# Layer norm output in four steps, and stage-end norms in row halves on two engines

## What is computed

```python
# first block (one layer)
h = h + y @ w_out[l]                       # y: two self attentions of rmsnorm(h), each normed
h = h + memory_cross_attention(rmsnorm(h, g_cross[l]), rmsnorm(mem, g_mem[l]), ...)
h = h + conv_ffn(rmsnorm(h, g_ffn[l]), ...)
# second block, per layer and stream
def conformer_conv(a, conv_w, conv_b, norm_g, norm_b, w_o):
    gl = a[..., :CONV_WIDTH_2] * jax.nn.sigmoid(a[..., CONV_WIDTH_2:])
    y = lax.conv_general_dilated(gl, ...) + conv_b
    y = jax.nn.silu(layer_norm(y, norm_g, norm_b))
    return y @ w_o
...
x = x + g1 * rms_norm(y, mix_post_g[l])    # y: the three branches merged, @ w_out
h2 = modulate(rms_norm(x, ffn_pre_g[l]), sh2, sc2)
x = x + g2 * rms_norm(sq_relu_mlp(h2, w_ff1[l], w_ff2[l]), ffn_post_g[l])
```

## Time and profile before

| | us |
|---|---|
| median of three runs | 2168.87 (2168.05 to 2169.55) |
| profiled execution | 2166.35 |
| its span, first to last instruction | 2164.4 |
| PE busy in the span | 2076.0 (96%) |
| DVE busy | 1464.7 (68%) |
| ACT busy | 1098.5 (51%) |
| mean granted TensorE clock | 0.989 of full |

### The profile page before, as it was taken

One profiled execution on the slowest core, in us unless ns is written; L12 is line 12 of the kernel. 1 busy time (PEld: TensorE's weight loads), 2 busy tenths in 40 slices (PEclk: granted clock), 3 DMA queues, 4 the chain that ended last, 5 costly groups with the idle time before them and its releaser, 6 DMA issues.

```text
span 2164.4 us, 32492 instructions
## 1 busy us (share of the span) xinstructions
PE 2076.0 (96%) x12953; PEld 1753.1 (81%) x12953; DVE 1464.7 (68%) x2181; ACT 1098.5 (51%) x1469; POOL 191.1 (9%) x376
## 2 busy tenths in 40 slices
PE   7999989999999999999999999999989999997997
PEld 6776879888877678887767888898978877777996
DVE  5666466577667778767767855575777677776555
ACT  5554444445565355567436544454555674354443
POOL 3100000110003300000500000000000014000000
PEclk9999999999999999999999999999999999999999
DMA  8645467666667745644664477666555446554653
GB/s 264 217 147 198 149 228 249 230 187 201 225 207 222 237 162 183 192 145 149 195 221 157 156 219 228 214 193 191 172 176 177 138 149 181 168 172 139 193 185 107
DMA packets 214245, 407.18 MB, mean 188 GB/s; under 512 B 19735, under 2 KB 22483, under 8 KB 214096
## 3 DMA queue, kind: packets, MB, share of 16 engines
q1 hardware_dynamic: 200352, 388.03, 56.1%
q0 software_dynamic: 13744, 17.08, 2.8%
HBM read 397.27 MB, written 1.30 MB: 184 GB/s over the span
## 4 chain that ended last, share of the span: by engine, by line
PE 82%; DVE 9%; ACT 5%; issue 3%; DMA 1%; DVEq 0%; ACTq 0%; SPq 0%
PE gps L1173 15%; PE gps L1175 14%; PE gps L1174 14%; PE gps L1180 9%; PE gps L1181 9%; PE gps L1182 9%; PE aps L997 2%; PE aps L1124 2%; DVE wlo L1990 2%; PE aps L1096 2%; PE aps L953 1%; ACT whi L1502 1%; ACT Yc L1383 1%; DMA raw<-ada_w 1%; PE aps L1105 0%
## 5 line engine op out<-in xcount | busy, mean ns | idle before, releaser
L1990 DVE TENSOR_TENSOR wlo<-raw,whi 128x1024 fp32r<-128x1024 f32 (+1 forms) x648 | 762.9, 1186 | 524.6 <-ACT whi L1502 522.6
L1502 ACT ACTIVATE whi<-raw 128x1024 fp32r<-128x1024 f32 (+1 forms) x648 | 662.2, 1028 | 668.7 <-PE gps L1175 444.1
L1173 PE MATMUL gps<-whi,ohi 128*128 128x512 f32 x1624 | 656.0, 404 | 16.9 <-DVE wlo L1990 12.7
L1174 PE MATMUL gps<-wlo,ohi 128*128 128x512 f32 x1624 | 635.8, 392 | 0.0
L1175 PE MATMUL gps<-whi,olo 128*128 128x512 f32 x1624 | 635.7, 391 | 0.0
L1180 PE MATMUL gps<-ohi,whi 128*128 128x256 f32 x1760 | 507.6, 288 | 3.8 <-issue 3.8
L1181 PE MATMUL gps<-olo,whi 128*128 128x256 f32 x1760 | 499.2, 284 | 0.0
L1182 PE MATMUL gps<-ohi,wlo 128*128 128x256 f32 x1760 | 498.8, 283 | 0.0
L1173 PEld LDWEIGHTS gps<-whi,ohi 128*128 128x128 f32 x1624 | 306.3, 189 | 107.4 <-issue 30.6
L1175 PEld LDWEIGHTS gps<-whi,olo 128*128 128x128 f32 x1624 | 306.6, 189 | 66.5
L1180 PEld LDWEIGHTS gps<-ohi,whi 128*128 128x128 f32 x1760 | 338.7, 192 | 21.9 <-issue 21.0
(11 more groups left out here) (287 smaller groups left out, 1504.2 us busy)
## 6 DMA issues: line engine op xcount, KB each, us to landing
raw<-w_in SPq DMA_DIRECT2D x232, 512.0 KB, 4.1
raw<-w_ff SPq DMA_DIRECT2D x192, 512.0 KB, 4.0
raw<-ada_w SPq DMA_DIRECT2D x96, 512.0 KB, 4.5
raw<-w_attn_o SPq DMA_DIRECT2D x24, 512.0 KB, 3.5
raw<-w_gmlp_o SPq DMA_DIRECT2D x24, 512.0 KB, 4.3
raw<-w_conv_o SPq DMA_DIRECT2D x24, 512.0 KB, 3.9
raw<-w_out SPq DMA_DIRECT2D x24, 512.0 KB, 4.6
raw<-w_gate SPq DMA_DIRECT2D x20, 512.0 KB, 4.5
```

What stands on the lines that cost most here:

```text
L1173: mm(om, ah, whi[:, q, i, :], start=first, stop=False)
L1174: mm(om, ah, wlo[:, q, i, :], start=False, stop=False)
L1502: A_(part(whi, jb, q), raw_part(jb, q), ACT.Copy).then_inc(hi_done[q], 1)
L1990: tt(part(wlo, jb, q), raw_part(jb, q), f32(part(whi, jb, q)), ALU.subtract).then_inc(lo_done[q], 1)
```

## The change

- `ln_out` becomes four steps per half: scale and tanh (ACT), multiply (DVE), `ohi` (ACT), `olo` (DVE), put at four units one apart or equal: half 0 at gates[4] 2, 3, 3 and gates[5] 0, half 1 at gates[5] 0, 1, 1 and 2. The steps on ACT are late, those on DVE are not.
- At j_ob[1] and j_mb[1] the add to the stream comes one unit earlier in DVE's list (`front`, ahead of the split of unit 2) and in two row halves. The squares of the first 512 columns, which the job before has already written, are taken ahead (`pn_half`), only the last 512 columns at the end.
- At these two places and in `ffn` of the last layer the second row half is scaled on ACT (`pn_x`), the first on DVE (`share`).
- Post norms: for `ycp` DVE multiplies the second row half first, while ACT squares the first, and ACT waits for `y_m1` before it squares the second. For `accy` the add is in two row halves, the squares start after the first, and the product with the gain goes to another buffer (`qT`), so that it doesn't wait for ACT.
- Five semaphores of the setup are merged into two (not shown in the diff).

```diff
+    def half_squares(jb, wait_job):
+
+        return put(jb, 1, "pn_half", after={"act": [("res_done", wait_job, 1, 1)]})
+
     def cross_norm(col, jb, wait_job):
-        st = put(jb, 0, "pn_stat", res="x", xn="RB",
+        wait_job.front = True
+        st = put(wait_job, 3, "pn_stat", res="x", xn="RB", share=True, early_half=half_squares(wait_job, j_ob[0]),
                  after={"act": [("res_done", wait_job, 1, 1)], "dve": []})
+        put(jb, 0, "pn_x", of=st)
         return transposed(jb, 2, "RB", 0, [("pn_xn", st, 2, 2)], scale=("C1", col))
 
     t_c = cross_norm(24, j_vm1, j_ob[1])
...
-    st_f = Step("pn_stat", res="x", xn="RB", after={"act": [("res_done", j_mb[1], 1, 1)], "dve": []})
+    st_f = Step("pn_stat", res="x", xn="RB", share=True, early_half=half_squares(j_mb[1], j_mb[0]), after={"act": [("res_done", j_mb[1], 1, 1)], "dve": []})
...
-    ups[0].gate.aux[0].append(st_f)
+    j_mb[1].aux[3].append(st_f)
+    j_mb[1].front = True
+    put(ups[0].gate, 0, "pn_x", of=st_f)
     ups[0].gate.aux[0].append(t_f)
...
-        lo = [put(jb, q, "ln_out", of=lm, l=l, slot=b_, half=h) for h, (jb, q) in enumerate(((gates[4], 3), (gates[5], 1)))]
+        lo = []
+        for h, (at_out, at_mul, at_hi, at_lo) in enumerate((((gates[4], 2), (gates[4], 3), (gates[4], 3), (gates[5], 0)),
+                                                            ((gates[5], 0), (gates[5], 1), (gates[5], 1), (gates[5], 2)))):
+            y = put(*at_out, "ln_out", of=lm, l=l, half=h)
+            put(*at_mul, "ln_mul", of=y, half=h)
+            put(*at_hi, "ln_hi", of=y, slot=b_, half=h)
+            lo.append(put(*at_lo, "ln_lo", of=y, slot=b_, half=h))
...
+                        if name == "pn_xn" and x.share and m:
+                            pe.wait_ge(sem["pn_xa"], x.shares)
+                        else:
+                            wait(pe, ev(name, x, 2, m + 1) if name == "pn_xn" else ev(name, x, per, i))
...
-                wait(act, *p.after["act"])
+                if p.early_half:
+                    act.wait_ge(sem["res_m0"], p.early_half.n + 1)
+                else:
+                    wait(act, *p.after["act"])
                 x, junk = rows(res[p.res]), rows(flat[p.xn])
+                j = slice(NW, D) if p.early_half else slice(0, D)
                 for m in range(2):
+                    if p.early_half and m:
+                        wait(act, *p.after["act"])
                     if p.po:
                         wait(act, ev("po_x", p.po, 2, m + 1))
-                    A_(junk[:, m, :], x[:, m, :], ACT.Square, accum_out=st[:, p.n % 2, m:m + 1]).then_inc(sem["pn_ss"], 1)
+                    A_(junk[:, m, j], x[:, m, j], ACT.Square, accum_out=st[:, p.n % 2, m:m + 1]).then_inc(sem["pn_ss"], 1)
+
+            def pn_x(p):
+                p = p.of
+                act.wait_ge(sem["pn_r"], p.shares)
+                A_(rows(flat[p.xn])[:, 1, :], rows(res[p.res])[:, 1, :], ACT.Identity, scale=st[:, 7 + p.n % 2, 1:2],
+                   bias=0.0).then_inc(sem["pn_xa"], 1)
+
+            def pn_half(p):
+                wait(act, *p.after["act"])
+                x, junk = rows(res["x"]), rows(RB)
+                for m in range(2):
+                    A_(junk[:, m, 0:NW], x[:, m, 0:NW], ACT.Square, accum_out=st[:, 14, 2 * (p.n % 2) + m:2 * (p.n % 2) + m + 1])
...
-                wait(act, ev("ln_r", p))
+
+            def ln_hi(p):
+                half = slice(p.half * 4 * S, (p.half + 1) * 4 * S)
+                wait(act, ev("ln_r", p.of))
                 A_(ohi[:, p.slot, 4 * p.half:4 * p.half + 4, :], tiles(RB[:, half], 4), ACT.Copy,
                    scale=0.5).then_inc(sem["ln_hi"], 1)
...
-                return p.kind == "conv0" or p.kind == "ada" and not p.early
+                return p.kind in ("conv0", "ln_out", "ln_hi") or p.kind == "ada" and not p.early
...
                 for m in range(2):
+                    if jb.evac == "accy":
+                        act.wait_ge(sem["y_add"], 2 * jb.n + m + 1)
+                    elif m:
+                        act.wait_ge(sem["y_m1"], jb.n + 1)
                     A_(Pb[:, m, :], src[:, m, :], ACT.Square,
                        accum_out=st[:, 5, 2 * jb.j + m:2 * jb.j + m + 1]).then_inc(sem["y_sq"], 1)
...
-                w = rms(p.n % 2, 2, 1.0 / D)
+                if p.early_half:
+                    e = 2 * (p.early_half.n % 2)
+                    link(tt(st[:, p.n % 2, 0:2], st[:, p.n % 2, 0:2], st[:, 14, e:e + 2], ALU.add))
+                w = rms(p.n % 2, 2, 1.0 / D, ready=p.shares if p.share else None)
                 x, y = rows(res[p.res]), rows(flat[p.xn])
+                if p.share:
+                    ts(y[:, 0, :], x[:, 0, :], w[:, 0:1], None, ALU.mult).then_inc(sem["pn_xn"], 2)
+                    return
                 for m in range(2):
                     ts(y[:, m, :], x[:, m, :], w[:, m:m + 1], None, ALU.mult).then_inc(sem["pn_xn"], 1)
...
-            def ln_out(p):
+            def ln_mul(p):
+                half = slice(p.half * 4 * S, (p.half + 1) * 4 * S)
+                wait(dve, ev("ln_th", p.of))
+                stt(RB[:, half], RB[:, half], 1.0, Yc[:, half], ALU.add, ALU.mult).then_inc(sem["ln_r"], 1)
+
+            def ln_lo(p):
                 half, ks = slice(p.half * 4 * S, (p.half + 1) * 4 * S), slice(4 * p.half, 4 * p.half + 4)
-                wait(dve, ev("ln_th", p))
-                stt(RB[:, half], RB[:, half], 1.0, Yc[:, half], ALU.add, ALU.mult).then_inc(sem["ln_r"], 1)
-                wait(dve, ev("ln_hi", p))
+                wait(dve, ev("ln_hi", p.of))
                 stt(olo[:, p.slot, ks, :], tiles(RB[:, half], 4), 0.5, f32(ohi[:, p.slot, ks, :]), ALU.mult,
...
-                tt(x, x, tiles(g, 2), ALU.add).then_inc(sem["res_done"], 1)
+                if jb.front:
+                    for m in range(2):
+                        t = tt(x[:, m, :], x[:, m, :], tiles(g, 2)[:, m, :], ALU.add)
+                        t.then_inc(sem["res_m0"], 1) if m == 0 else t.then_inc(sem["res_done"], 1)
+                else:
+                    tt(x, x, tiles(g, 2), ALU.add).then_inc(sem["res_done"], 1)
...
+            def gained(jb):
+
+                return "RB" if jb.evac == "ycp" else "qT"
+
             def gain(jb, src):
 
                 j = slice(jb.j * NW, (jb.j + 1) * NW)
                 dve.wait_ge(sem["gb_in"], 16 * jb.gb)
-                for m in range(2):
-                    dve.wait_ge(sem["y_sq"], 2 * jb.y + m + 1)
-                    t = tt(rows(RB)[:, m, j], src[:, m, :], GB[:, j], ALU.mult)
-                t.then_inc(sem["y_cp"], 1)
+                y = rows(flat[gained(jb)])
+                if jb.evac == "ycp":
+                    dve.wait_ge(used[NQ - 1], jb.i + 1)
+                    tt(y[:, 1, j], src[:, 1, :], GB[:, j], ALU.mult).then_inc(sem["y_m1"], 1)
+                    dve.wait_ge(sem["y_sq"], 2 * jb.y + 1)
+                    tt(y[:, 0, j], src[:, 0, :], GB[:, j], ALU.mult).then_inc(sem["y_cp"], 1)
+                else:
+                    tt(y[:, 0, j], src[:, 0, :], GB[:, j], ALU.mult)
+                    tt(y[:, 1, j], src[:, 1, :], GB[:, j], ALU.mult).then_inc(sem["y_cp"], 1)
                 for p in jb.then:
                     po(p)
...
                 dve.wait_ge(used[NQ - 1], jb.i + 1)
                 y = rows(RB)[:, :, jb.j * NW:(jb.j + 1) * NW]
                 wait(dve, ("ac_add", jb.before, 1, 1))
-                tt(y, y, tiles(g, 2), ALU.add).then_inc(sem["y_add"], 1)
-                dve.wait_ge(sem["y_add"], jb.n + 1)
+                for m in range(2):
+                    tt(y[:, m, :], y[:, m, :], tiles(g, 2)[:, m, :], ALU.add).then_inc(sem["y_add"], 1)
+                dve.wait_ge(sem["y_add"], 2 * (jb.n + 1))
                 gain(jb, y)
...
-                    if q == NQ - 1 and jb.evac in evacs:
+                    if q == (NQ - 2 if jb.front else NQ - 1) and jb.evac in evacs:
```

More of the change, by code:

```diff
@@ L68, in __init__ @@
         self.po = args.get("po")
+        self.front = False
+        self.share, self.early_half = args.get("share"), args.get("early_half")
         self.glu, self.tile, self.cks = (args.get(k) for k in ("glu", "tile", "cks"))
@@ L257, in make_plan, with prenorm @@
     d2 = down(2, ups[4:6], 6)
-    def prenorm(jb, q, jt, qt, l, s, which, xn, slot, wait=(), po=None):
-        st = put(jb, q, "pn_stat", res=s, xn=xn, after={"act": wait, "dve": wait}, po=po)
+    def prenorm(jb, q, jt, qt, l, s, which, xn, slot, wait=(), po=None, share=False):
+        st = put(jb, q, "pn_stat", res=s, xn=xn, after={"act": wait, "dve": wait}, po=po, share=share)
+        if share:
+            put(jb, q, "pn_x", of=st)
         return transposed(jt, qt, xn, slot, [("pn_xn", st, 2, 2)], scale=("gs", l, s, which), shift=("sh", l, s, which))
@@ L520, in make_plan @@
                     bank[b] = ("t_lo", p, 4, b + 1)
+            elif k == "pn_stat":
+                p.shares = count["shares"] = count.get("shares", 0) + bool(p.share)
```

(21 more changed lines are left out.)

41 lines of the change are left out of this document (20 added, 21 removed).

## The result

| | before | after |
|---|---|---|
| median | 2168.46 us (2166.59 to 2169.55, 4 runs) | 2150.27 us (2149.36 to 2152.91, 4 runs) |
| profiled execution, span | 2166.35, 2164.4 | 2151.05, 2149.3 |

The ratio is 0.9921, 95% interval 0.9909 to 0.9933: faster by 18 us, 15 to 20. The prediction said 2153.4 (2149 to 2159). The medians lie 18.2 apart, the profiled executions 15.3; the prediction's 15.5 was a sum for the latter.

What follows compares the result with a forecast made beforehand. PE was busy 2076 of 2164.4 us, so only shortening its waits or the chain behind its last matmul could count. Terms 10.2 + 3.0 + 0.8 - 0.1 + 1.6 = 15.5 us gave 2153.4, range 2149 to 2159.

Steps and rivals of the forecast that it cites:

- Layer norm output, 3.75 per mixer and 1.0 back in the first: Waits at three layer norm outputs: 4.4 us less 0.65 each, 1.0 of new wait in the first mixer; 10.2 in all.
- the walk had 0.65: ACT and DVE lists followed with measured durations: at the layer norm output, co.1's copy comes 0.65 us late for PE.
- Stage ends, 3.0: Behind j_mb[1] and j_ob[1]: the chain to the transposes gets 1.5 us shorter at each, 3.0 together.
- Last mixer, 0.8: Behind the last mixer: 0.65 us from the gain's opposite half order, 0.2 from the second scaling on ACT.
- 9.6 instead of 10.48: Sign of being right: transposes behind the last mixer start after a wait of 9.6 us instead of 10.48.
- The scaling on ACT, taken as 1.06: Second row half scaled on ACT at three places: 1.06 us assumed, between 1.01 and 2.07.
- Late `ycp`, -0.1: Second `ycp` of the middle mixer: ACT waits for a late DVE, the chain slips by 0.1 us.
- Post norms, 1.6: Feed forward post norms: gain follows the add without waiting for ACT, 0.8 us at program end and 0.8 at 1597.70.
- The clock did not fall: Rival: the clock falls all the same behind small waits, 3.8 to 5.7 us back, 2157.2 to 2159.1; chance 0.15.
- Nor did it help: Rival: an untouched wait of this size, shifted, may draw no clock fall, 1.9 us more, 2151.5; chance 0.15.
- The slower rival: Layer norm output: each unit pays the round trip between engines, 4.57 us against 2.7 of PE; 2178.6; chance 0.03.
- I take the difference as the same for both: Last step: profiled execution lies 2.5 us under the median 2168.87 before, and the same after, giving 2153.4.

Runs made afterwards that it cites:

- second profile of before: The kernel before, unchanged, timed and profiled again: 2167.82 us against 2168.13 (24 runs of before).
- slower twin: Changed kernel with the layer norm's ACT steps ahead of the weight copy of their unit instead of behind it: 2169.73 us against 2151.79.
- second comparison: The changed kernel itself once more against the kernel before: 2151.79 us against 2167.37, ratio 0.9925, 15.6 us.
- that one word in a list: Changed kernel with DVE's attention norm scaling (`ynM`) taken out of `LATE`, so ahead of its unit's weight copy: 2141.11 us, 0.9874 of before.

## Why the prediction was right

- *Layer norm output, 3.75 per mixer and 1.0 back in the first.* Right by mechanism and by size (3.74, 3.77, 3.74, and 1.07 back in the first). The waits left read 0.34 to 0.36 where the walk had 0.65, but from start to start two units take 6.09 us instead of 5.45, so they cost 0.64. The second profile of before shows that 4.4 us was the right price of the old waits at either clock. The walk of both lists with measured durations is what told the changed kernel from its slower twin.
- *Stage ends, 3.0.* Right in sum, 3.15, but the working gave the credit to the wrong piece. The half squares, for which I booked squares done at 285.4 instead of 287.42, give 0.27, because they delay the add, and 1.1 come from the place of the add. I had counted that delay (0.5) without asking what the chain would be without them.
- *Last mixer, 0.8.* It gave 0.62: the order of the halves 0.46 instead of 0.65, the scaling the 0.2. The sign "9.6 instead of 10.48" didn't come: the wait reads 10.09, and the other 0.23 come between the first and the second half of the transposes. In these rows of the last `ycp` ACT's second square waits for DVE's first product, and DVE's small steps wait for that square:
```profile
1945.01 0.69 DVE L2002 TENSOR_TENSOR RB<-gps,GB 128x512 f32<-128x512 f32 x1 [0.41 <-PE gps L1198]
...
1945.73 0.60 ACT L1510 ACTIVATE QP<-gps 128x512 f32<-128x512 f32 x1
...
1946.52 0.16 DVE L1648 TENSOR_TENSOR st<-st 128x2 f32<-128x2 f32 x1 [0.17 <-ACT QP L1510]
```
- *The scaling on ACT, taken as 1.06* within 1.01 to 2.07, is 1.15; the squares of the same 1024 columns, in the kernel before, take 1.06:
```profile
285.20 1.06 ACT L1217 ACTIVATE RB<-xres 128x1024 f32<-128x1024 f32 x1 [1.09 <-DVE xres L1875]
```
```profile
285.97 1.15 ACT L1251 ACTIVATE RB<-xres,st 128x1024 f32<-128x1024 f32 x1 [1.29 <-DVE st L1602]
```
The Trainium skill (ScalarE: Activation LUTs, "What ACT_TABLE_LOAD costs") has 93 ns per pointer operand; the two rows agree.
- *Late `ycp`, -0.1.* The mechanism was right, the place wrong: nothing in the middle mixer, 0.2 behind the first.
- *Post norms, 1.6.* They gave 1.6. At the end, the small steps begin 2.65 us behind the start of the add instead of 3.49; before:
```profile
2153.30 1.22 DVE L1943 TENSOR_TENSOR RB<-RB,gps 128x1024 f32<-128x1024 f32 x1 [6.03 <-PE gps L1175]
...
2156.79 0.16 DVE L1590 TENSOR_TENSOR st<-st 128x2 f32<-128x2 f32 x1
```
and now:
```profile
2138.98 1.28 DVE L2019 TENSOR_TENSOR RB<-RB,gps 128x512 f32<-128x512 f32 x2 [6.53 <-PE gps L1198]
...
2141.63 0.16 DVE L1648 TENSOR_TENSOR st<-st 128x2 f32<-128x2 f32 x1
```
- *The rivals.* The clock did not fall behind the small waits of 0.33 to 0.82, in either profile. Nor did it help: behind the untouched wait of 2.2, now at 1184.84, it fell in both (0.66 and 0.52 in the 3 us from 1184). The slower rival did not come, but one line away it does.
- *The step that was off* is the last: "I take the difference as the same for both". The first comparison's medians are 18.2 apart. 1.8 of the missing 2.7 are the profiled execution of before, which lies that much under its median of 24 runs; the second comparison gave 15.6. What differs between the two profiles of before is mostly the clock: the 1.6 us behind the second wait of the first mixer, which I counted nowhere because the first profile lacked it, stands in the second. How often it comes in unprofiled runs, and so how much of the 18.2 it is, stays open. The sum of places was better than one comparison of four runs could show.

## What to carry over

Where two engines hand work back and forth inside an in-order list of independent copies, put each waiting half-step behind a copy and not ahead of one, and walk both lists with measured durations: between the same four cuts on either side of the copies lie some 18 us. Look next for steps that stand behind a copy although their input has long been there; that one word in a list was worth 10 us. A piece that shortens a chain but stands ahead of something the chain needs should be tried without.
